# A transformer pair on one core: constant products put into seven more waits of TensorE

## The chip, the cores and the metric

The kernel runs on one core of one Trainium2 chip. The metric is the time on the device in microseconds (us) from the launch of the program to its end; smaller is better. A core has TensorE (matrix products, "PE" in the profile; its weight loads are "PEld"), VectorE ("DVE"), ScalarE ("ACT"), GpSimd ("POOL"), SyncE ("SP", here a queue that issues DMAs) and 16 DMA engines. TensorE reads from the on-chip memory SBUF and writes to eight banks of a second memory, PSUM, which the other engines read. TensorE's clock is granted at one of two levels, 2.4 GHz (the profile writes 1.00) and 1.2 GHz (0.50), and the profile tells which of them was granted over any stretch.

## The reference, cut to what matters

Everything is float32. Two different models are run one after the other on 512 tokens of width 1024:

```python
# first part: 2 layers on 16 meta tokens + 512 tokens
for l in range(2):
    u = rms_norm(h, ln_mix[l])
    (aq, ak, av, bq, bk, bv, cq, ck, cv, dq, dzf, dzb, di, dg, gz) = split_in(u @ w_in[l])
    y_a = windowed_sink_attention(...)     # softmax attention A, 4 heads
    y_b = axial_rope_attention(...)        # B
    y_c = differential_attention(...)      # C: two softmaxes, p1 - lam * p2
    y_d = hgrn2_bidirectional(...)         # linear attention, forwards and backwards
    merged = sum(sigmoid(gz)[n] * (y @ w_branch[l, n]) for n, y in ...)
    h = h + merged @ w_out[l]
    u = rms_norm(h, ln_ffn[l])
    h = h + (silu(u @ w_ffn_gate[l]) * (u @ w_ffn_up[l])) @ w_ffn_down[l]
x = rms_norm(h, ln_final)[meta:]
# second part: one layer, modulated by c
x = x + 0.5 * ga1 * rms_norm(swiglu(modulate(rms_norm(x, g), sh1, sc1), ...))
...                                        # window attention, S5 state space, w_out
x = x + 0.5 * ga3 * rms_norm(swiglu(modulate(rms_norm(x, g), sh3, sc3), ...))
```

The output is x. Nothing in the change touches a value of it.

## The kernel before, in words

Each engine has its own program, written out in order, and the programs meet at semaphores: `pe.wait_ge(S["x"], n)` holds TensorE's next instruction, and all behind it, until the counter x has reached n. TensorE's program is a fixed sequence. Activations lie with features on the partitions and the 528 tokens (16 meta, 512 others) along the free axis, in five token tiles (four of 128 and, last, the one of 16 meta tokens; `NT` is 5). A large product is done in three products of a high and a low half (`split_lin`, L1382 to L1384), with the weights streamed from HBM into a ring of slots; ScalarE makes the high half (L2243) and VectorE the low half (L2935) of each.

**The softmax attention** is `attention(first, end, turns, l)`, called once for each layer of the first part. It loops over steps n from `first` to `end + 1`. A step's unit `att[n]` is one pair of heads of one token tile of one kind; the kinds come in the order C, A, B, with 10 units each in layer 0 (so n is 0 to 29 and `end` is 30) and 8 each in layer 1, which has no meta tile left (30 to 53, `end` 54). In step n TensorE makes the scores of unit n (`scores`, L1644 and L1651), the values of unit n-2 (`values`, L1696 and L1710: these need the probabilities turned and copied out of PSUM by ScalarE, L2517), and turns the probabilities of unit n-1 (`turn_probs`, L1681 and L1684: after ScalarE's exponentials, L2503). Between them go `fill_piece`s, independent pieces of the input projection of 24 matmuls (L1733 to L1744), which give TensorE work while the others compute. The last two steps have no fill. Scores go to banks 0 to 3 (kinds A and B: banks 2(n mod 2) and the next); VectorE's minimum over them (L3285, semaphore `att_min`) frees them. `cell_end(n)` is the count of `att_min` at which unit n's scores have been read. The last unit of B ends in ScalarE's copy (L2526) and VectorE's scaling (L3359, `y_ready`).

**The linear attention** `linear_attention(ly)` first waits for that `y_ready`, then makes a `gate_piece` (L1835 to L1837: 24 matmuls of 264 or 256 columns and six more), then `head_stats` (L1807: matmuls of two columns), another gate piece, and so on. Its loop goes over units (d, t), direction and token tile; each has `sums` (L1880), two `pairs` (L1901), `outputs`, `state`, with gate pieces as fills (`fill`) between. `pairs(n, hp)` waits for factors that VectorE and GpSimd make (`g_query_x`, `g_key_x`; GpSimd's part is L500) and for `g_masked`, which says that banks 2 and 3 have been read. The unit (1, 4), direction 1 with the meta tile, is there in layer 0 alone, as its ninth.

**The second part's front** is `ffn(b2["ffn1"], ssm=True)`; its first two jobs are `pair_lin` (L1616 to L1619), which takes the eight tiles of x one by one as ScalarE (L2382) and VectorE (L2921) finish them, after the normalisation that ends the first part (`joint_means`, L1482 to L1487).

**Constant products.** `idle_products(bank, count)` multiplies `ident` (128x128) by 264 columns of constants into a bank that nothing reads before it is written anew:

```python
def idle_products(bank, count):
    for _ in range(count):
        mm(PS[:, bank, 0:264], ident, con[:, 0:264], start=True, stop=True)   # L1469
```

Before, it is called at the start of each layer only (L2013 to L2023), 62 matmuls in all.

Of the kernel before, what the change touches and what calls it, by code (L numbers as in the profile page):

```python
# [37 lines left out]
NT = len(TILES)  # L38
# [238 lines left out]
def build(nc, ins, out_dram):  # L277
    with ExitStack() as ctx:
# [259 lines left out]
        S = {n: sem(n) for n in names}  # L538
# [292 lines left out]
        layers = []  # L831
        x_there = [(x_loaded[k // 2], 16) for k in range(KT)]
        h_there = x_there
        for l in range(DEPTH):
            ly = dict(l=l)
# [112 lines left out]
        att, groups = [], []  # L948
# [94 lines left out]
        def cell_end(n):  # L1043

            return att[n]["cell0"] + len(att[n]["cells"])
# [319 lines left out]
        def _(pe):  # L1365
# [100 lines left out]
            def idle_products(bank, count):  # L1466

                for _ in range(count):
                    mm(PS[:, bank, 0:264], ident, con[:, 0:264], start=True, stop=True)  # L1469

            def mean_square(n):

                for i in range(len(n["tiles"])) if n["total"] is None else (0, KT - 1):
                    mean_tile(n, i)
# [129 lines left out]
            def pair_lin(js, x):  # L1604

                for j in js:
                    wait(pe, jobs[j.n - NB].freed)
                    pe.wait_ge(S["w_low"], j.loads[0].s + 1)
                for i in range(KT):
                    for part in range(2):  # L1610
                        wait(pe, x["is_low" if part else "is_high"][i])
                        for j in js:
                            (a, z), (wh, wl, xh, xl) = j.pieces[0], j.terms[i]
                            out = PB[j.buf][:, 0, 0:z - a]
                            if part == 0:
                                mm(out, wh, xh[:, a:z], start=i == 0, stop=False)  # L1616
                                mm(out, wl, xh[:, a:z], start=False, stop=False)
                            else:
                                last = mm(out, wh, xl[:, a:z], start=False, stop=i == KT - 1)  # L1619
                                if i == KT - 1:  # L1620
                                    last.then_inc(lin_full[j.buf], 1)
# [154 lines left out]
            def attention(first, end, turns=None, l=0, gated=False):  # L1776
                if gated:
                    scores(att[first])
                for n in range(first, end + 2):
                    if n < end and not gated:  # L1780
                        if n == turns:
                            pe.wait_ge(S["b_heads_ready"], NT * (l + 1))
                        scores(att[n])
                        made_scores[0] = n + 1
                    if first <= n - 2:
                        values(att[n - 2])
                    if first <= n - 1 < end:
                        turn_probs(att[n - 1], 0)
                        if second_bank(n - 1) != 4:
                            turn_probs(att[n - 1], 1)  # L1790
                    for f in fills_at.get(n, ()) if n < end else ():
                        fill_piece(f)
                    if gated:
                        if n + 1 < end:
                            scores(att[n + 1])
                        gated_step(n - first)
                    if first <= n - 1 < end and second_bank(n - 1) == 4:
                        turn_probs(att[n - 1], 1)
                    if turns and 0 <= n - layers[l]["turn_step"] < NT:
                        turn_heads(l, n - layers[l]["turn_step"])  # L1800
# [23 lines left out]
            def gate_piece(ly, q):  # L1824

                n, k, s, i = q // 16, q // 2 % KT, q % 2, NPIECE * ly["l"] + q
                ld, xu, xy = ly["gw"][q // 2], ly["xu"], ly["xy"][n]
                a, z = ly["cuts"][s]

                def terms(out, first, xs, seen=()):  # L1830
                    for m, (xh, xl) in enumerate(xs):
                        if seen:
                            wait(pe, seen[m])
                        wh, wl = high(ld)[:, first + m, :], low(ld)[:, first + m, :]
                        mm(out, wh, xh[:, a:z], start=m == 0, stop=False)  # L1835
                        mm(out, wh, xl[:, a:z], start=False, stop=False)  # L1836
                        last = mm(out, wl, xh[:, a:z], start=False, stop=m == len(xs) - 1)  # L1837
                    return last

                pe.wait_ge(S["w_low"], ld.s + 1)  # L1840
                if i:
                    pe.wait_ge(S["piece_gate"], i)
                terms(PS[:, 6, 0:z - a], 0, tiles_of(xu, range(KT)), xu["is_low"] if q == 0 else ()
                      ).then_inc(S["piece_full"], 1)
                if i:
                    pe.wait_ge(S["piece_read"], i)
                terms(PS[:, 7, 0:z - a], KT, tiles_of(xy, range(2)), xy["is_low"] if q % 16 == 0 else ()
                      ).then_inc(S["piece_branch"], 1)

            def linear_attention(ly):  # L1850
# [4 lines left out]
                pe.wait_ge(S["log_low"], NT * (l + 1))  # L1855
                pe.wait_ge(S["fill_read"], FILLS[l + 1])
                made = [3]
                gate_piece(ly, 0)
                head_stats("c", l, SQC, tiles[:NT - l])
                gate_piece(ly, 1)  # L1860
# [21 lines left out]
                                      RR[d][0:rows, 4 * i:4 * i + 4, 0:rows], start=x is LZH, stop=x is LZL)  # L1882
                    last.then_inc(S["g_sums"], 1)

                def pairs(n, hp):

                    u, d, t, a, z, rows = kept_of(n)
                    key, query = (0, HALF) if d == 0 else (HALF, 0)
                    pe.wait_ge(S["g_key_x"], 2 * u + hp + 1)
                    pe.wait_ge(S["g_query_x"], 2 * u + hp + 1)  # L1890
                    if 2 * u + hp:
                        pe.wait_ge(S["g_masked"], 2 * u + hp)
                    for plane in range(planes(rows)):
                        for b, w in blocks(rows):
                            for i in range(2):
                                out, lo = PS[b:b + w, 2 + i, HALF * plane:HALF * plane + w], HALF * i
                                if plane:
                                    x = y = EB[hp][lo:lo + HALF, plane - 1, b:b + w]
                                else:
                                    x, y = KF[lo:lo + HALF, hp, b:b + w], DQ[hp][lo:lo + HALF, a + b:a + b + w]  # L1900
                                last = mm(out, x, y, start=True, stop=True)  # L1901
                    if rows == P:
                        for i in range(2):
                            x = EB[hp][HALF * i:HALF * i + HALF, NLEV - 1, :]
                            last = mm(PS[key:key + HALF, 2 + i, HALF * NLEV:P * 4], x[:, key:key + HALF],
                                      x[:, query:query + HALF], start=True, stop=True)
                    last.then_inc(S["g_pairs"], 1)
# [42 lines left out]
                for n in range(len(units_of[l])):  # L1950
                    u, d, t, a, z, rows = kept_of(n)
                    if u:
                        pe.wait_ge(S["g_kf"], u)
                        pe.wait_ge(S["g_ez"], u)
                    for hp in range(2):
                        turn(PS[:, 5, 256 + P * hp:256 + P * hp + rows],
                             KTM[0:rows, t, 256 * d + P * hp:256 * d + P * hp + P], ident[0:rows, 0:rows])
                    mm(PS[0:rows, 5, 0:256], ZR[d][0:rows, 0:rows], LZH[0:rows, t, 256 * d:256 * d + 256],
                       start=True, stop=False)
                    mm(PS[0:rows, 5, 0:256], ZR[d][0:rows, 0:rows], LZL[0:rows, t, 256 * d:256 * d + 256],  # L1960
                       start=False, stop=True).then_inc(S["g_z"], 1)
                    sums(n, 0)
                    fill(n, 0)
                    if n:
                        if kept_of(n - 1)[5] == P:
                            outputs(n - 1, 1, HALF, False)
                        state(n - 1)
                    sums(n, 1)
                    fill(n, 1)
                    pairs(n, 0)  # L1970
                    fill(n, 2)
                    pairs(n, 1)
                    carried(n)
                    outputs(n, 0, 0, True)
                    fill(n, 3)
                    if rows == P:
                        outputs(n, 0, HALF, False)
                    fill(n, 4)
                    outputs(n, 1, 0, True)
# [2049 lines left out]
```

## Time and profile before

| what | value |
|---|---|
| time, median of 3 runs | 2984.65 us (2983.28 to 2986.08) |
| span of the profiled execution, first to last instruction | 2989.1 us |
| mean granted TensorE clock over that span | 0.992 |
| TensorE busy | 2927.0 us (98%) |
| VectorE, ScalarE, GpSimd busy | 1900.7 (64%), 1134.5 (38%), 377.3 us (13%) |

The time of the profiled execution as a whole is not given; what is known of it is its span of 2989.1 us, which is 4.45 us above the median of the timed runs.

How to read the rows below. In a timeline a row gives start and duration in us, engine, line and operation, tiles, shape, the number of instructions merged into the row, and in brackets the engine's idle time before it with what ended that. A matmul's duration includes its way through the pipeline, so the cost of one of several is the distance of their starts, or the row's duration over its count. In a table of stretches a row gives the stretch in us, its length, then for PE, PEld, DVE, ACT and POOL the busy time with the number of instructions, then the granted TensorE clock (1.00 is 2.4 GHz), the DMA engines' share and GB/s. Where the table was asked for PE alone, only PE's column stands before the clock.

### The profile page before, as it was taken

The page shows a single profiled execution, that of the slowest core. Times are in us where ns is not written, and L with a number is a line of the kernel's source. Part 1 is how long each engine was busy: PE and PEld are TensorE (multiplying, and loading weights), DVE is VectorE, ACT ScalarE, POOL GpSimd, SP SyncE. Part 2 cuts the span into 40 slices and gives each one's busy share as a digit, 9 for nine tenths or more (in the row PEclk, how much of TensorE's full clock was granted, in tenths as well). Part 3 has the DMA queues.
Part 4 walks back from the last instruction along what each step waited for, and adds up shares of the span by engine and source line. Part 5 has one row for each costly group of instructions (what it writes and reads, how often), then busy time and mean ns, then how long its engine had stood idle before and what let it go on. Part 6 is the DMA issues. An engine that isn't in the chain of part 4 may idle for free.

```text
span 2989.1 us, 56782 instructions
## 1 busy us (share of the span) xinstructions
PE 2927.0 (98%) x23600; PEld 2632.0 (88%) x23600; DVE 1900.7 (64%) x3660; ACT 1134.5 (38%) x2022; POOL 377.3 (13%) x610
## 2 busy tenths in 40 slices
PE   9999999999999999999999999999999999999998
PEld 8777999999999998789999899987888885799997
DVE  5564677557777746646865766677536655685565
ACT  4655233232212235552323434434222222554353
POOL 0242433000000020323320000002000000000000
PEclk9999999999999999999999999999999999999999
DMA  6725766244555574347533444438723431134442
GB/s 207 212 49 143 182 149 165 73 141 158 196 189 169 196 213 127 72 131 190 148 114 121 151 143 152 162 115 214 185 93 135 141 121 43 57 115 157 148 174 85
DMA packets 119511, 428.65 MB, mean 143 GB/s; under 512 B 14248, under 2 KB 16680, under 8 KB 114264
## 3 DMA queue, kind: packets, MB, share of 16 engines
q1 hardware_dynamic: 67032, 261.50, 25.6%
q0 software_dynamic: 52224, 163.51, 20.7%
q8 instruction: 189, 3.10, 0.4%
q14 instruction: 66, 0.54, 0.1%
HBM read 414.34 MB, written 109.01 MB: 175 GB/s over the span
## 4 chain that ended last, share of the span: by engine, by line
PE 88%; DVE 4%; ACT 4%; issue 2%; DMA 1%; POOL 1%; SPq 0%; DVEq 0%; ACTq 0%; POOLq 0%
PE acc L1382 13%; PE acc L1383 13%; PE acc L1384 13%; PE acc L1835 5%; PE acc L1836 5%; PE acc L1837 5%; PE acc L2101 4%; PE acc L2102 4%; PE acc L2103 4%; ACT temps L2503 2%; PE acc L1710 2%; PE acc L1651 1%; PE acc L1417 1%; PE acc L2119 1%; PE acc L1901 1%
## 5 line engine op out<-in xcount | busy, mean ns | idle before, releaser
L2243 ACT ACTIVATE toep_r<-ring 128x1024 fp32r<-128x1024 f32 (+2 forms) x216 | 251.4, 1165 | 327.6 <-PE acc L1384 327.6
L1383 PE MATMUL acc<-normed_r,toep_r 128*128 128x264 f32 (+2 forms) x1120 | 357.0, 319 | 0.0
L2935 DVE TENSOR_TENSOR ring_r<-ring,toep_r 128x1024 fp32r<-128x1024 f32 (+2 forms) x212 | 289.4, 1366 | 96.1 <-ACT toep_r L2243 95.5
L1384 PE MATMUL acc<-work_r,ring_r 128*128 128x264 f32 (+2 forms) x984 | 323.6, 329 | 0.0
L1835 PE MATMUL acc<-residual_r,toep_r 128*128 128x264 f32 (+1 forms) x1024 | 301.0, 294 | 1.6 <-DVE mixed L3359 1.6
L1836 PE MATMUL acc<-normed_r,toep_r 128*128 128x264 f32 (+1 forms) x1024 | 292.2, 285 | 0.0
L1837 PE MATMUL acc<-residual_r,ring_r 128*128 128x264 f32 (+1 forms) x1024 | 291.3, 284 | 0.0
L1382 PE MATMUL acc<-work_r,toep_r 128*128 128x264 f32 (+2 forms) x828 | 268.4, 324 | 0.6 <-DVE ring_r L2945 0.6
L1383 PE MATMUL acc<-work_r,toep_r 128*128 128x264 f32 (+2 forms) x720 | 231.5, 321 | 0.0
L1383 PEld LDWEIGHTS acc<-normed_r,toep_r 128*128 128x128 f32 x1120 | 210.6, 188 | 14.5
L1835 PEld LDWEIGHTS acc<-residual_r,toep_r 128*128 128x128 f32 x1024 | 195.5, 191 | 8.0 <-DVE mixed L3359 1.9
L1382 PE MATMUL acc<-mixed_r,toep_r 128*128 128x264 f32 x704 | 202.5, 288 | 0.0
L1384 PEld LDWEIGHTS acc<-work_r,ring_r 128*128 128x128 f32 x984 | 185.1, 188 | 17.3
L1384 PE MATMUL acc<-mixed_r,ring_r 128*128 128x264 f32 x704 | 199.5, 283 | 0.0
L1836 PEld LDWEIGHTS acc<-normed_r,toep_r 128*128 128x128 f32 x1024 | 195.7, 191 | 1.5
L2649 ACT ACTIVATE toep<-acc 128x264 f32<-128x264 f32 (+1 forms) x128 | 49.6, 388 | 386.8 <-PE acc L1837 386.8
L1837 PEld LDWEIGHTS acc<-residual_r,ring_r 128*128 128x128 f32 x1024 | 196.1, 192 | 0.0
L1382 PEld LDWEIGHTS acc<-work_r,toep_r 128*128 128x128 f32 x828 | 155.7, 188 | 13.7 <-issue 1.2
L1382 PE MATMUL acc<-temps_r,toep_r 128*128 128x512 f32 (+1 forms) x416 | 157.0, 377 | 0.7 <-DVE ring_r L2935 0.7
L1384 PE MATMUL acc<-temps_r,ring_r 128*128 128x512 f32 (+1 forms) x416 | 155.4, 374 | 0.0
L2503 ACT ACTIVATE temps<-temps,small 128x528 f32<-128x528 f32 (+6 forms) x176 | 113.3, 644 | 91.0 <-DVE small L3285 90.8
L1383 PEld LDWEIGHTS acc<-work_r,toep_r 128*128 128x128 f32 x720 | 135.4, 188 | 10.5
(614 smaller groups left out, 8117.3 us busy)
## 6 DMA issues: line engine op xcount, KB each, us to landing
ring<-in_w_pair SPq DMA_DIRECT2D x120, 512.0 KB, 3.8
sums_store<-in_w_pair POOLq DMA_DIRECT2D x80, 512.0 KB, 8.8
ring<-in_w_gb SPq DMA_DIRECT2D x64, 640.0 KB, 4.5
ring<-in_w_down SPq DMA_DIRECT2D x32, 704.0 KB, 4.2
lower_store<-in_w_pair POOLq DMA_DIRECT2D x20, 1024.0 KB, 10.4
sums_store<-sums_store POOLq DMA_DIRECT2D x40, 512.0 KB, 5.1
extra<-in_w_ada POOLq DMA_DIRECT2D x18, 1024.0 KB, 6.0
toep<-in_w_ada POOLq DMA_DIRECT2D x18, 1024.0 KB, 6.3
```

The source lines that it names most:

```text
L1382: mm(out, wh, xh[:, a:z], start=i == 0, stop=False)
L1383: mm(out, wh, xl[:, a:z], start=False, stop=False)
L1384: last = mm(out, wl, xh[:, a:z], start=False, stop=end)
L1835: mm(out, wh, xh[:, a:z], start=m == 0, stop=False)
L1836: mm(out, wh, xl[:, a:z], start=False, stop=False)
L1837: last = mm(out, wl, xh[:, a:z], start=False, stop=m == len(xs) - 1)
L2101: mm(out, wh, xh, start=begins and k == 0, stop=False, skip_group_check=True)
L2102: mm(out, wh, xl, start=False, stop=False, skip_group_check=True)
L2103: last = mm(out, wl, xh, start=False, stop=k == 3, skip_group_check=True)
L2243: A(high(ld), slot(ld), ACT.Copy).then_inc(S["w_high"], 1)
L2503: A(x, x, ACT.Exp, bias=negm[0:rows, i:i + 1], scale=-1.0, accum_out=sums[0:rows, i:i + 1]).then_inc(S["att_exp"], 1)
L2935: V.tensor_tensor(low(ld), slot(ld), high(ld), ALU.subtract).then_inc(S["w_low"], 1)
```

## The change

`idle_scores(n, count)` is new: it waits until the scores of unit n have been read and then puts `count` constant products into the first of their banks. Constant products are added in seven places, 31 matmuls in all. `pairs` waits for `g_masked` first instead of last. Nothing is taken away, and no other engine's program is changed.

```diff
+            def idle_scores(n, count):
+                pe.wait_ge(S["att_min"], cell_end(n))
+                idle_products(2 * (n % 2), count)
...
 def pair_lin(js, x):                      # second part's front
                 for j in js:
                     wait(pe, jobs[j.n - NB].freed)
                     pe.wait_ge(S["w_low"], j.loads[0].s + 1)
+                idle_products(2 * js[0].buf, 5)
                 for i in range(KT):
...
 def attention(...):
                 for n in range(first, end + 2):
+                    if n == first + 1 and not gated:
+                        if l:
+                            pe.wait_ge(S["y_ready"], layers[0]["groups"])
+                        idle_products(6, 3)
+                    if n == end + 1 and not gated:
+                        idle_scores(end - 2, 3)
                     if n < end and not gated:
                         ...
                         scores(att[n])
...
                         if second_bank(n - 1) != 4:
                             turn_probs(att[n - 1], 1)
+                    if n == layers[l]["A"][0] and l == 0 and not gated:
+                        idle_scores(n - 1, 3)
+                    if n == end and not gated:
+                        idle_scores(end - 1, 2)
                     for f in fills_at.get(n, ()) if n < end else ():
...
 def linear_attention(ly):
                 pe.wait_ge(S["y_ready"], ly["groups"])
                 ...
                 made = [3]
+                idle_scores(ly["B"][1] - 1, 2)
                 gate_piece(ly, 0)
...
-                def pairs(n, hp):
+                def pairs(n, hp, unread=0):
+                    if 2 * u + hp:
+                        pe.wait_ge(S["g_masked"], 2 * u + hp)
+                    if unread:
+                        idle_products(2, unread)
                     pe.wait_ge(S["g_key_x"], 2 * u + hp + 1)
                     pe.wait_ge(S["g_query_x"], 2 * u + hp + 1)
-                    if 2 * u + hp:
-                        pe.wait_ge(S["g_masked"], 2 * u + hp)
...
-                    pairs(n, 0)
+                    pairs(n, 0, 3 if (d, t) == (1, NT - 1) else 0)
```

## Rows read from the trace of the kernel before

**Rows 1.** The page's parts 1 and 4: busy time; chain that ended last, by engine.
```profile
PE 2927.0 (98%) x23600; PEld 2632.0 (88%) x23600; DVE 1900.7 (64%) x3660; ACT 1134.5 (38%) x2022; POOL 377.3 (13%) x610
PE 88%; DVE 4%; ACT 4%; issue 2%; DMA 1%; POOL 1%; SPq 0%; DVEq 0%; ACTq 0%; POOLq 0%
```
**Rows 2.** The view of cores: span and mean granted TensorE clock.
```profile
core 0: 2989.1 us, clock 0.992
```
**Rows 3.** Table of stretches, all engines: the seven at 1.2 GHz inside the span.
```profile
174.50:181.20 6.70, 6.70 (x46) 6.24 (x43) 6.10 (x19) 1.72 (x7) 3.42 (x4) 0.50 0.00 1
...
287.20:297.30 10.10, 9.51 (x82) 9.22 (x81) 0.67 (x2) 1.89 (x6) 0.00 (x0) 0.50 0.01 2
300.80:304.10 3.30, 3.30 (x17) 3.30 (x16) 0.00 (x0) 0.00 (x0) 3.30 (x2) 0.50 0.00 0
...
505.60:512.30 6.70, 5.99 (x45) 5.98 (x46) 3.42 (x17) 0.00 (x0) 4.02 (x9) 0.50 0.63 193
1160.95:1164.30 3.35, 2.88 (x14) 2.83 (x15) 3.28 (x12) 1.94 (x5) 0.00 (x0) 0.50 0.01 2
1314.55:1317.90 3.35, 3.35 (x27) 2.61 (x23) 0.22 (x2) 0.77 (x1) 2.44 (x1) 0.50 0.03 5
2027.95:2031.30 3.35, 3.35 (x8) 2.66 (x9) 3.35 (x6) 1.88 (x3) 0.00 (x0) 0.50 1.11 198
```
**Rows 4.** Timeline of PE, the kernel's start: constant products that are already there.
```profile
3.21 5.34 PE L1469 MATMUL acc<-con 128*128 128x264 f32 x14 [3.21 <-DMA con<-in_consts]
9.12 3.83 PE L1469 MATMUL acc<-con 128*128 128x264 f32 x16 [0.57 <-ACT work L2200]
```
**Rows 5.** Timeline of PE, front of layer 1's softmax attention: unit 31's scores, unit 30's turns.
```profile
1158.17 0.43 PE L1644 MATMUL acc<-con,work 128*128 128x64 f32 x2 [0.52 <-DVE small L3285]
...
1161.42 0.59 PE L1681 MATMUL acc<-con,temps 128*16 128x128 f32 x2 [1.74 <-DVE temps L3301]
```
**Rows 6.** Table of stretches, PE alone: like stretches of layer 0 and of layer 1.
```profile
107.73:112.03 4.30, 4.12 (x35) 1.00 1.06 129
1161.42:1166.68 5.26, 5.26 (x35) 0.72 0.00 0
107.73:129.70 21.97, 20.85 (x201) 1.00 0.73 155
1161.42:1183.63 22.21, 21.80 (x201) 0.93 0.12 39
```
**Rows 7.** Timeline of PE, layer 0, step 10: second half of unit 9's turns; next fill.
```profile
172.78 0.39 PE L1684 MATMUL acc<-con,temps 16*128 16x16 f32 x4 [1.07 <-ACT mixed L2517]
...
176.42 0.55 PE L1742 MATMUL acc<-toep_r,residual_r 128*128 128x256 f32 x1
```
**Rows 8.** Timeline of PE, layer 0's last units and the first gate piece.
```profile
286.99 0.98 PE L1710 MATMUL acc<-mixed,work 128*64 128x16 f32 x16 [1.26 <-ACT mixed L2517]
...
289.22 0.61 PE L1696 MATMUL acc<-con,small 16*64 16x16 f32 x8
289.76 1.04 PE L1710 MATMUL acc<-mixed,work 128*64 128x16 f32 x16
...
291.72 0.59 PE L1835 MATMUL acc<-residual_r,toep_r 128*128 128x264 f32 x1 [0.59 <-DVE mixed L3359]
```
**Rows 9.** Timeline of PE, layer 1's last units.
```profile
1314.26 1.77 PE L1710 MATMUL acc<-mixed,work 128*64 128x128 f32 x16 [2.01 <-ACT mixed L2517]
...
1318.41 0.66 PE L1696 MATMUL acc<-con,small 128*64 128x128 f32 x8
1319.45 1.09 PE L1710 MATMUL acc<-mixed,work 128*64 128x128 f32 x16 [0.38 <-ACT mixed L2517]
```
**Rows 10.** Timeline of PE, layer 0's linear attention, ninth unit: pairs and gate piece.
```profile
506.31 0.45 PE L1901 MATMUL acc<-work 64*16 64x16 f32 x20 [1.12 <-POOL work L500]
506.69 0.59 PE L1835 MATMUL acc<-residual_r,toep_r 128*128 128x264 f32 x1
```
**Rows 11.** Timeline of PE, the second part's front: the first product.
```profile
2027.86 0.73 PE L1616 MATMUL acc<-temps_r,toep_r 128*128 128x512 f32 x1 [2.21 <-ACT temps_r L2382]
```

## The prediction

> **What bounds the kernel now.** I read the page's busy times and its chain first. TensorE is busy 98% of the span and holds 88% of the chain that ended last [rows 1]; the reader should take from this that the end moves with TensorE's own work and with the few microseconds in which it stands still, and that nothing is won on another engine unless TensorE waits for it. Then the view of cores: the mean granted clock is 0.992 over 2989.1 us [rows 2], so about 0.008 x 2989.1 x 2 = 48 us passed at 1.2 GHz. The table of stretches finds those inside the span [rows 3]: seven, together 36.9 us, for 35.1 us of which TensorE is busy; the rest, as far as the rounding goes, lies at the very end, where TensorE has nothing left to do. All seven begin in or just behind a wait or a run of very small matmuls. The timelines around them show what TensorE did before the clock fell, and what each new product will lie beside.
>
> What is to be had at most follows from rows 3. Where TensorE runs dense products at 1.2 GHz, half of the busy time would go. Where it runs small matmuls less goes: the 16 matmuls of L1710 took 1.77 us at 1.2 GHz and 1.09 us at 2.4 [rows 9]. All seven stretches gone would save about 3.0 (174.5) + 3.5 (287.2) + 1.6 (300.8) + 2.8 (505.6) + 1.0 (1161) + 1.4 (1314.6) + 1.6 (2028) = 14.9 us. TensorE's page in the Trainium skill ("TensorE: Matmul & The Clock Gate", Terms) prices it otherwise: the throttled time times one minus the clock's share. By that page the same 36.9 us would be worth an estimated 18.4 us; the L1710 rows disagree (0.68 us saved of 1.77, where the page gives 0.89), because small matmuls are paced by more than the clock.
>
> **The price of a product.** 16 constant products took 3.83 us at 2.4 GHz, 0.24 us each; 14 at the start, where the clock was still low, took 5.34 us, 0.38 us each [rows 4]. I take these two. 31 products are 7.4 us at 2.4 GHz if nothing hides them. The waits added are all for things read long before: `att_min` of a unit whose turns are already made, layer 0's `y_ready` in layer 1, `g_masked` of a mask whose outputs are already under way. I cost the waits at nothing; behind them in TensorE's queue is everything, so if one was late its whole lateness would be on the path.
>
> **The seven places.**
>
> *Step first+1, both layers, 3 products (0.72 us).* They go before the scores of the second unit, which stand 0.52 us idle for VectorE's minimum [rows 5]; a little more is hidden by the tail of the fill before it, so they end at most 0.2 us late. The scores themselves are followed by 1.74 us of idleness that ends with VectorE's work on the unit before [rows 5]. The 0.2 is thus hidden there: cost 0. In layer 1 the clock fell at the end of that second wait, 0.5 us ahead of the turns; in layer 0, with the same waits, it did not. The two layers price the fall: from the turns to the next scores it is 4.30 us in layer 0 and 5.26 in layer 1, 0.96 us more; but at the next wait for VectorE's L3301 it is 21.97 against 22.21, 0.24 us more [rows 6], since VectorE, not TensorE, set that point and TensorE waited less for it. The gain lies between 0.2 and 1.0; I take 0.3.
>
> *Step A[0], layer 0, 3 products.* They go into the 1.07 us before the second half of unit 9's turns [rows 7]. 0.72 us is hidden wholly: cost 0. The clock fell 1.7 us later [rows 3], after a stretch of matmuls of 16 columns. From 176.42 to 181.2 the fill ran dense at 1.2 GHz [rows 7], so 4.8 / 2 = 2.4 us are to be had, and 0.6 in the small ones before. If the three products hold the clock, up to 3.0; the steps behind it wait now and then for ScalarE, so I take 2.4 when it is held; and I take it as held at 6 in 10: 1.4.
>
> *End of the softmax attention, 2 + 3 products, and 2 more before the first gate piece.* Here I argue against the change. The waits that stand out, 1.26 us in layer 0 and 2.01 us in layer 1, are before the values of the last unit but one [rows 8, 9]. The new products come behind these values and behind the last unit's turns, immediately one after the other, before L1696. In layer 0 there is no idle time between L1696 and the last values [rows 8]: five products are 5 x 0.38 = 1.9 us, all on the path, as the clock is already low from 287.2 on. In layer 1 L1696 is followed by 0.38 us of idleness for ScalarE's copy [rows 9], so 1.2 - 0.4 = 0.8 us are on the path. The last two stand behind the wait for `y_ready`, not in it, so nothing hides them: 0.8 us in layer 0 at 1.2 GHz, 0.5 in layer 1. Against that, seven products in a thin stretch let the clock come back sooner after the fall, before the gate pieces: from 291.72 to 297.3, 5.6 us, these ran at 1.2 GHz, and a start that is 2.7 us later leaves about 2.9 us of them there: 1.3 us won back. Layer 0: 2.7 - 1.3 = +1.4, between -0.8 (clock back before the last values) and +2.7; I take +1.0. Layer 1: the stretch at 1.2 GHz ends before the new products: +1.3, between 0 (a fall behind it is avoided in other executions) and +1.3; I take +1.2. The stretch at 300.8 follows the two-column matmuls of `head_stats`; no product is put there: 0, and between -1.6 and 0.
>
> *pairs, unit (1, 4), 3 products.* They go into the 1.12 us for GpSimd [rows 10], hidden; cost 0. The clock fell 0.7 us before that wait ended [rows 3], so only about half of the products can come before it. The gate piece from 506.69 to 512.3 ran at 1.2 GHz [rows 10]: 2.8 us if held. Even chances: 1.4 less a little for the unit's own latencies, 1.2.
>
> *pair_lin, 5 products (1.2 us).* They go into the 2.21 us before the first product, hidden. The clock fell 0.1 us behind that wait [rows 11, 3]. Eight products of 512 columns took 3.35 us there, 0.42 us each where half would do: 1.6. VectorE, which makes the tiles, was busy for all of the 3.35 us too [rows 3], so it could hold TensorE up once that is faster; I take 1.5, between 0.3 and 1.7.
>
> **The sum.** -0.3 -1.4 +1.0 +1.2 -1.2 -1.5 = -2.2 us; with some relief for stretches that fall in other executions (layer 0's front did not fall in this one) I put it at -2.5. The sum is made against the profiled span of 2989.1 us, which would become 2986.6; that execution lies 4.45 us above the median, and as the clock falls at somewhat different places in each, I carry the difference to the median: 2984.65 - 2.5 = 2982.1.
>
> **The rivals.**
>
> *All of it works (0.25).* The clock is held at all four waits that are filled, and the products at the ends of the softmax attention bring it back early or keep it up. For it: four of the seven falls stand at waits that are filled, and two more at the ends. Against it: at both ends the longest wait stays empty. Gains 1.0 + 3.0 + 2.8 + 1.6, layer 0's end -0.8, the stretch at 300.8 -1.6, layer 1's end 0: about -10.8, or 2974; a milder form of it, -7, gives 2977.6.
>
> *The others take over (0.20).* TensorE gets to its next wait sooner and stands longer there, as in rows 6, where three quarters of the loss was gone 22 us later. Then the gains shrink to a quarter except in the second part's front: -0.25 -0.6 -0.6 -1.5 + 2.2 = -0.8: 2983.9.
>
> *The ends decide (0.15), slower than before.* The seven products at the end of each softmax attention are on the path at full price, 2.7 + 1.3 = 4.0 us, the clock comes back no sooner, and the filled waits hold the clock only in the second part's front (-1.5) or not even there. For it: the place of the products behind the long wait, and 287.2 to 297.3 at 1.2 GHz already. It decides as soon as fewer than two of the three other stretches are saved. +2.5 to +4.0: 2987.2 to 2988.7, and past 2990.6 only where the later start brings one more fall onto dense work (another 1.6 to 3).
>
> *The products don't move the clock at all.* It is within the last one; the constant products at the kernel's start ran from 0.38 down to 0.24 us each as the clock was granted [rows 4], which speaks against it. It would leave the costs alone, +2.2 to +4.0.
>
> **The numbers.** The forecast's own case has 0.40. Changes under 0.2% (6 us) can hardly be told from none here. Faster by over 0.2%, under 2978.7: most of the first rival and a little of the forecast's, 0.26. Slower by over 0.2%: 0.06. Within: 0.68. The range of 8 in 10 goes from 2975.5 to 2987.5.
>
> **What would show it.** In the profile after: at 2027 to 2031 a clock of 1.00 and products of L1616 0.23 us apart; 31 more matmuls of L1469; the idle times before L1644 in the front and before L1684 at 172, L1901 at 506 and L1616 at 2027 filled; at the ends the last values starting 0.7 us or more later behind the turns than before, and the first gate piece two products behind `y_ready`. I am wrong if the ends cost nothing (then ScalarE's copy or VectorE ended last there), if the clock falls again a few microseconds behind a filled wait, or if the mean granted clock stays at 0.992.

## The result: 0.19% slower

Over 21 runs of each on the same chips the changed kernel took 2992.44 us in the median (2989.25 to 2999.96) and the kernel before 2987.38 us (2980.82 to 2995.20). The ratio is 1.0019, with a 95% interval of 1.0013 to 1.0025: 5.7 us slower, 3.9 to 7.5. The forecast was 2982.1 us, 0.09% faster than the 2984.65 us of the three runs shown then, in a range up to 2987.5. The sign was wrong. (Those three runs of before were also low ones: with more of them its median is 2987 to 2989 us. This moves both kernels alike and is not the error: 5.7 us on top of 2984.65 would be 2990.4, outside the range too.)

The clock did what was hoped for. The mean granted clock, averaged over the runs, rose from 0.9925 (34 runs of before) to 0.9958 (21 runs of the change): 2 x 0.0075 x 2988 = 45 us at 1.2 GHz became 25 us. Twenty microseconds of low clock went, and the kernel became slower. So the products cost more than they brought.

The profile after, first the view of cores and TensorE's line of the page's part 1, which answer to [rows 1, 2]:

```profile
core 0: 2990.6 us, clock 0.996
```
```profile
PE 2933.3 (98%) x23662; PEld 2635.4 (88%) x23662; DVE 1900.7 (64%) x3660; ACT 1134.2 (38%) x2022; POOL 376.2 (13%) x610
```

The other engines are unchanged. TensorE has 62 more instructions than in [rows 1], not 31. The view of line L1469 in the trace of before, and then in that of after, says why (after the count: shortest, median and longest duration in ns, then the first and last start in us):

```profile
L1469 PE MATMUL acc<-con x62: 386/386/809, 3.2 to 1075.8; 128*128 128x264 f32 x62
```
```profile
L1469 PE MATMUL acc<-con x124: 384/386/807, 3.5 to 2033.0; 128*128 128x264 f32 x124
```

Before, the code calls `mm` on this line 31 times (7 + 4 x 2 + 6 in layer 0, 2 + 8 in layer 1), and the trace has 62 matmuls. A product of two full float32 operands is two instructions here. The change adds 31 calls of `mm`, which the description of it counts as 31 matmuls, and thus 62 instructions of 0.24 us: **a call costs 0.48 us, not 0.24.** The row that I took the price from said x14 where the code beside it says 7.

The stretches at 1.2 GHz that the profile after has inside its span, in the table of stretches (columns as in [rows 3]), and two stretches that lost theirs:

```profile
287.70:291.00 3.30, 3.30 (x10) 2.54 (x10) 0.00 (x0) 0.38 (x3) 0.00 (x0) 0.50 0.02 5
301.35:304.70 3.35, 3.35 (x17) 3.35 (x16) 0.00 (x0) 0.00 (x0) 3.35 (x3) 0.50 0.00 0
506.15:509.50 3.35, 3.35 (x30) 2.33 (x29) 3.24 (x18) 0.00 (x0) 2.64 (x7) 0.50 0.14 49
1160.95:1164.30 3.35, 3.03 (x27) 3.04 (x28) 3.17 (x11) 2.10 (x6) 0.00 (x0) 1.00 0.00 0
1315.10:1318.40 3.30, 3.30 (x17) 2.77 (x14) 0.00 (x0) 1.45 (x3) 2.85 (x1) 0.50 0.00 0
1366.30:1369.65 3.35, 3.35 (x19) 3.35 (x17) 1.85 (x10) 0.00 (x0) 3.35 (x11) 0.50 0.47 92
2027.95:2035.00 7.05, 6.54 (x23) 3.99 (x22) 3.60 (x6) 3.58 (x6) 4.05 (x4) 1.00 0.93 177
```

Seven stretches of 36.9 us became five of 17 us. The falls at 174, 1161 and 2028 are gone, those at 287 and 506 are shorter, those at 301 and 1315 are as they were, and there is a new one at 1366. Each profile is one execution; which of these differences are the change's is read from all thirteen profiles, at the end of the experiments. The stretch at 287.7 holds nothing but ten instructions of L1469: the clock was low while the kernel multiplied constants.

**The ends of the softmax attention**, in the timeline of after, layer 0 (answering to [rows 8]):

```profile
286.31 0.65 PE L1716 MATMUL acc<-mixed,work 128*64 128x16 f32 x16 [1.26 <-ACT mixed L2536]
...
287.75 4.12 PE L1469 MATMUL acc<-con 128*128 128x264 f32 x10
291.80 0.41 PE L1702 MATMUL acc<-con,small 16*64 16x16 f32 x8
...
293.59 1.16 PE L1469 MATMUL acc<-con 128*128 128x264 f32 x4 [0.59 <-DVE mixed L3378]
294.39 0.48 PE L1851 MATMUL acc<-residual_r,toep_r 128*128 128x264 f32 x1
```

and layer 1 (answering to [rows 9]):

```profile
1313.85 1.09 PE L1716 MATMUL acc<-mixed,work 128*64 128x128 f32 x16 [2.01 <-ACT mixed L2536]
...
1317.44 2.90 PE L1469 MATMUL acc<-con 128*128 128x264 f32 x10
1320.28 0.66 PE L1702 MATMUL acc<-con,small 128*64 128x128 f32 x8
...
1323.18 1.16 PE L1469 MATMUL acc<-con 128*128 128x264 f32 x4 [1.01 <-DVE mixed L3378]
```

The reader should see three things. The long waits, 1.26 and 2.01 us, stand exactly as before; the products come after them. Ten instructions take 4.12 us where the clock is low and 2.90 where it comes back on the way, 0.8 and 0.6 us a call. And four more stand behind the wait for `y_ready`. The first gate piece starts at 294.39 where before it started at 291.72, although the values before it started 0.68 us earlier: 3.35 us lost up to there. The earlier rise of the clock gave back 2.4: the matmuls of `head_stats` behind the gate piece start at 298.23, against 297.99 before, 0.9 us late by the same measure. In layer 1 the values start 0.41 us earlier than before and the gate piece (1323.98 against 1321.92) 2.06 later, 2.5 us lost.

**The overfull waits**, in the timeline of after (to [rows 7, 10, 11]):

```profile
172.60 1.60 PE L1469 MATMUL acc<-con 128*128 128x264 f32 x6
174.13 0.42 PE L1690 MATMUL acc<-con,temps 16*128 16x16 f32 x4
...
505.70 2.65 PE L1469 MATMUL acc<-con 128*128 128x264 f32 x6
508.28 0.45 PE L1920 MATMUL acc<-work 64*16 64x16 f32 x20
...
2031.04 2.39 PE L1469 MATMUL acc<-con 128*128 128x264 f32 x10
```

Three calls fill 1.5 us where the wait had 1.07, and 2.6 us where it had 1.12, since there the clock fell in their midst. These waits are gone from the profile, as forecast. I had the first two filled to two thirds, and they ran over by 0.4 and 1.4 us; in the second part's front ten instructions took 2.39 us in a wait of 2.21, and the first product came no later behind L1492 (before, L1487) than before. In the front of the softmax attention the scores came 0.66 us later behind the fill, but the wait behind them shrank from 1.74 to 1.18 us, so the turns came no later: cost 0, as forecast.

### The profile page after: what moved, and what is told of

Same layout as the page of the kernel before. It is cut to its first block, busy times and chain, and to the rows that moved or that the text cites. A ratio compares the mean times of both kernels' runs of the same rounds, so it can differ in the third digit from the quotient of the medians.

```text
span 2990.6 us, 56906 instructions
## 1 busy us (share of the span) xinstructions
PE 2933.3 (98%) x23662; PEld 2635.4 (88%) x23662; DVE 1900.7 (64%) x3660; ACT 1134.2 (38%) x2022; POOL 376.2 (13%) x610
## 4 chain that ended last, share of the span: by engine, by line
PE 88%; DVE 5%; ACT 4%; issue 2%; DMA 1%; POOL 1%; SPq 0%; DVEq 0%; ACTq 0%
PE acc L1382 13%; PE acc L1383 13%; PE acc L1384 13%; PE acc L1851 5%; PE acc L1852 5%; PE acc L1853 5%; PE acc L2120 4%; PE acc L2121 4%; PE acc L2122 4%; ACT temps L2522 2%; PE acc L1716 2%; PE acc L1657 1%; PE acc L1417 1%; PE acc L2138 1%; PE acc L1897 1%
## 5 line engine op out<-in xcount | busy, mean ns | idle before, releaser
L2954 DVE TENSOR_TENSOR ring_r<-ring,toep_r 128x1024 fp32r<-128x1024 f32 (+2 forms) x212 | 287.7, 1358 | 95.5 <-ACT toep_r L2262 94.9
L1383 PEld LDWEIGHTS acc<-normed_r,toep_r 128*128 128x128 f32 x1120 | 210.6, 188 | 14.5
```

The source lines that it names most:

```text
L2954: V.tensor_tensor(low(ld), slot(ld), high(ld), ALU.subtract).then_inc(S["w_low"], 1)
```

## The experiments

All ratios are against the kernel before, with 95% intervals, from 5 rounds each; "clock" is the mean granted clock over a kernel's runs. `pairs` waits for `g_masked` first in every one of these kernels, also in those that are otherwise the kernel before with one addition (e7, e8). In the runs of before beside them it was 0.9923 to 0.9930.

**e1: the waits alone.** The three lines at the ends are taken out of the change.

```diff
-                    if n == end + 1 and not gated:
-                        idle_scores(end - 2, 3)
-                    if n == end and not gated:
-                        idle_scores(end - 1, 2)
-                idle_scores(ly["B"][1] - 1, 2)
```

> The change without its products at the ends of the softmax attention (2 + 3 before the last values, 2 before the first gate piece); the fillings of the front, of step A[0], of pairs and of pair_lin stay, 17 calls. After the result (0.19% slower) three theories stand. PRICE: one call of idle_products is two matmul instructions (the trace of before has 62 for 31 calls), 0.48 us at 2.4 GHz and 0.76 at 1.2, so the ends cost twice what I took, all on the path, and the fillings still win. It expects 0.05 to 0.15% faster than before here (2 to 4 us), that is 7 to 9 us below the whole change. FEW FALLS: the profiled execution of before had more clock falls than most, so there is little for the fillings to win: within 0.05% of before. OTHERS: the fillings themselves do the harm, overfull waits (3 calls are 1.4 us in a wait of 1.07 or 1.12 us) or waits moved to other engines: 0.1% slower or more.

Measured: 0.9992 (0.9983 to 1.0000), median 2984.97 us against 2989.20, clock 0.9957. That is inside PRICE's range. The interval holds FEW FALLS' range too (within 0.05% of before); what speaks against FEW FALLS is its premise: over 34 runs the mean clock of before is 0.9925, so the profiled execution with its 0.992 was an ordinary one. OTHERS is refuted: the fillings don't harm. And the clock is that of the whole change (0.9957 against 0.9958): the fourteen calls at the ends bring no clock on top.

**e2: the ends alone.** The fillings in the front, at step A[0], in `pairs` and in `pair_lin` are taken out, the ends stay.

> The kernel before with only the products at the ends of the softmax attention, seven calls in each layer. PRICE: 7 x 0.76 = 5.3 us in layer 0 less 2 to 3 won back by an earlier rise of the clock, 7 x 0.48 to 0.76 less 0.4 idle in layer 1 = 3 to 5, less 1: 5 to 7 us slower, 0.17 to 0.23%. FEW FALLS: the same sum, 4 to 6 us. OTHERS: 0 to 2 us slower, under 0.07%.

Measured: 1.0018 (1.0009 to 1.0028), 5.4 us slower, clock 0.9937. Inside PRICE's range (and FEW FALLS', which has the same sum here); OTHERS expected under 0.07%. The ends alone are as slow as the whole change. Against e1 the change is 0.27% slower (1.0019 to 0.9992), 8 us for the same 14 calls, 0.58 us each. That they cost less alone may be because they then win some clock (0.9937 against 0.9925), but the two figures, 5.4 and 8 us, lie within each other's uncertainty.

**e5: the ends doubled.** As e2, each count twice.

```diff
-                        idle_scores(end - 2, 3)
+                        idle_scores(end - 2, 6)
-                        idle_scores(end - 1, 2)
+                        idle_scores(end - 1, 4)
-                idle_scores(ly["B"][1] - 1, 2)
+                idle_scores(ly["B"][1] - 1, 4)
```

> As e2 with the three counts at the ends of the softmax attention doubled, 4 + 6 before the last values and 4 before the first gate piece: 14 calls in each layer where e2 has 7. After the first four runs PRICE leads: a call is 0.48 us at 2.4 GHz and all on the path. The seven more calls in each layer run mostly when the clock is up again: 2 x 7 x 0.48 = 6.7 us above e2, +0.22% on top of its +0.18%, so +0.36 to +0.42%. Rival HIDDEN (the calls at the ends are partly hidden and e2's loss comes from more clock falls behind them): +0.20 to +0.30%. If a call cost what I took (0.24 us), +0.29%.

Measured: 1.0051 (1.0038 to 1.0064) in 5 runs, clock 0.9932. The point is above what each theory expected; the interval reaches into PRICE's range (0.36 to 0.42%) and stays clear of the other two. The 14 further calls cost 0.33%, 9.9 us or 0.7 us each, with an uncertainty of about 0.35 us on that. The timeline of e5, the last calls before each layer's last values:

```profile
289.51 7.06 PE L1469 MATMUL acc<-con 128*128 128x264 f32 x20
...
1321.85 4.62 PE L1469 MATMUL acc<-con 128*128 128x264 f32 x20
```

Twenty instructions, ten calls: 7.06 and 4.62 us. In layer 1, with the clock up, that is 0.46 us a call and 0.23 an instruction. HIDDEN and the price that I had taken are both refuted. The calls of the trace also add up to the loss: from their first start to the start of what follows it is 7.00 and 4.55 us for these twenty and 1.69 us in each layer for the four behind `y_ready`, less the 0.4 us of idleness that they fill in layer 1: 14.5 us, and 0.51% is 15.2 us, with a mean clock hardly above that of before (0.9932 against 0.9930). So the excess over PRICE is, in this trace, the 0.7 us that each of layer 0's ten calls took where the clock was down for most of them.

**e3: the products put into the wait that was left empty.** As e1, and two calls in layer 0, four in layer 1, ahead of the values of the last unit but one.

```diff
+                    if n == end and not gated:
+                        idle_scores(end - 2, 2 if l == 0 else 4)
                     if first <= n - 2:
                         values(att[n - 2])
```

> As e1, and 2 calls (layer 0) and 4 calls (layer 1) in the wait that the change leaves empty, ahead of the values of the last unit but one (1.26 and 2.01 us idle in the trace of before). PRICE: 2 x 0.48 fit into 1.26, 4 x 0.48 into 2.01; where they hold the clock the falls at 287 and 1315 go, 1 to 4 us below e1: 0.1 to 0.25% faster than before. FEW FALLS: not much different from e1, up to 2 us below. OTHERS: no gain over e1, or a loss.

Measured: 0.9980 (0.9971 to 0.9989), median 2982.32 us, clock 0.9963. Within PRICE's range. The timeline of e3 (layer 0, then layer 1):

```profile
283.94 1.16 PE L1469 MATMUL acc<-con 128*128 128x264 f32 x4
285.27 0.65 PE L1716 MATMUL acc<-mixed,work 128*64 128x16 f32 x16 [0.18 <-issue]
...
1304.84 1.95 PE L1469 MATMUL acc<-con 128*128 128x264 f32 x8
1307.01 1.09 PE L1716 MATMUL acc<-mixed,work 128*64 128x128 f32 x16 [0.23 <-issue]
```

The waits of 1.26 and 2.01 us are down to 0.18 and 0.23, and the values don't start later for it. The table of stretches of e3:

```profile
284.00:288.50 4.50, 3.77 (x63) 3.04 (x62) 0.76 (x3) 1.85 (x10) 0.00 (x0) 1.00 0.01 4
288.65:292.00 3.35, 3.35 (x16) 3.35 (x17) 0.38 (x1) 1.05 (x2) 0.00 (x0) 0.50 0.00 0
...
1305.00:1313.00 8.00, 6.48 (x67) 4.71 (x65) 2.07 (x5) 4.79 (x11) 2.90 (x1) 1.00 0.00 0
```

In layer 1 the clock stays up through the end. In layer 0, whose last units are matmuls of 16 columns, it still falls, here for 3.4 us. That isn't shown to be the filling's doing: the profile of e10, the same kernel, has 6.7 us there, and that of e8, which puts nothing there, has 3.3. The tables of stretches of e10 and e8:

```profile
287.20:293.90 6.70, 6.11 (x43) 5.97 (x40) 0.67 (x2) 1.38 (x3) 0.00 (x0) 0.50 0.01 2
290.10:293.40 3.30, 2.88 (x13) 2.88 (x14) 0.67 (x2) 1.25 (x3) 0.00 (x0) 0.50 0.02 5
```

In e3's profiled execution the fall at 288.65 is the only one before the last 10 us of the span; it was also the fastest of e3's 11 runs, 2977.4 us. That of e10 has five.

**e4: every count cut to what its wait holds**: 1, 2, 2 and 4 calls for 3, 3, 3 and 5, and e3's.

> As e3, with every count cut to what its wait holds at 0.48 us a call: 1 call in the front (0.52 us), 2 at step A[0] (1.07), 2 at pairs (1.12), 4 at pair_lin (2.21), 2 and 4 at the ends. PRICE: up to 1.5 us below e3 where the overfull waits cost (0.4 us at A[0] and up to 1.4 at pairs in the profile of after), unless the fewer products let the clock fall again: 0.1 to 0.3% faster than before. FEW FALLS: 0 to 0.05% faster. OTHERS: better than e3 by 1 to 2 us, since less is overfull.

Measured: 0.9986 (0.9977 to 0.9994), clock 0.9957. No better than e3, rather the other way, within the uncertainty. I had expected up to 1.5 us of gain. That what is saved on overfull waits is paid back in clock would fit the two clocks (0.9957 against 0.9963), but these lie within their scatter: not shown.

**e7: e3's addition alone**, on the kernel before (with the order of waits in `pairs` changed).

> The kernel before with only the products in the longest wait at the end of the softmax attention, ahead of the values of the last unit but one: 2 calls in layer 0, 4 in layer 1. PRICE (what fits into a wait costs nothing, and may hold the clock): -0.03 to -0.12%, what e3 has over e1 (0.12%) with its uncertainty. Rival: e3's lead over e1 was chance: 0 to +0.05%, since the clock falls a little later all the same.

Measured: 0.9995 (0.9984 to 1.0005), clock 0.9942. The point lies in PRICE's range, but the interval holds both theories: not decided by the time. The clock, 0.9942 against 0.9930, is hardly outside its scatter.

**e8: pair_lin's five calls alone** (and the order of waits in `pairs`).

> The kernel before with only the five calls of pair_lin. In the profile of after this place won 2.4 us against before. PRICE: 5 x 0.48 = 2.4 us in a wait of 2.2, the clock held: -1.6 to -2.4 us, -0.05 to -0.08%. OTHERS (VectorE takes it back at its next weight split): -0.02 to 0%.

Measured: 0.9997 (0.9987 to 1.0008), clock 0.9938. Inconclusive, between the two ranges: less than 2 us can't be told apart so. The single pieces of the gain were too small to be measured one at a time; together they are measured. The changed order of waits in `pairs` was never run by itself; e7 and e8 both have it and neither is slower than before by more than 0.08% at the end of its interval, so it is not what makes the change slower.

**e6: the change at the price that I had taken.** In the attention layers each call makes two one-instruction products instead of one float32 product:

```diff
+                for _ in range(2 * count):
+                    mm(PS[:, bank, 0:264], HR[:, 0, 0:P], HR[:, 0, 0:264], start=True, stop=True)
```

> The whole change, but each of the calls inside the attention layers (26 of the 31) makes two products of 264 columns in the short form that the fills use (one instruction each, about 0.12 us, both operands from the rounded activations) instead of one in full float32 (two instructions, 0.24 us each). So a call costs 0.24 us, the price that I took. The numbers of instructions and all waits are those of the change. PRICE: the ends then cost about half, 3 to 4 us less than the change, which comes out at my own sum: -0.02 to -0.12% against before. Rival PLACE (what counts is that something stands there at all: the waits, the order of pairs, clock falls), as the change: +0.1 to +0.2%.

Measured: 1.0011 (1.0001 to 1.0020), clock 0.9941. A miss: I had expected a gain. The ends did become cheaper; the timeline of e6, the ten short products before layer 0's last values, at low clock, where the change had 4.12 us:

```profile
290.64 2.57 PE L1479 MATMUL acc<-residual_r 128*128 128x264 f32 x10
```

But the clock was held less. The table of stretches of e6:

```profile
172.50:182.60 10.10, 10.10 (x70) 8.99 (x69) 8.33 (x25) 3.18 (x15) 4.46 (x4) 0.50 0.09 34
288.60:298.70 10.10, 9.51 (x82) 8.98 (x80) 0.67 (x2) 1.89 (x6) 0.00 (x0) 0.50 0.01 2
```

At step A[0], where the change lost its fall, there are 10 us at 1.2 GHz again. So my sum would have been wrong at my own price, too: with the cheap products the gain that I set against it didn't come.

**e9: the waits alone, with short products.**

> As e1 (the fillings without the ends), with the products inside the attention layers in the short form of e6: 9 of... all calls but pair_lin's five take half as long. e6 came out at +0.11% where I had expected a gain; its profile has the clock falling for 10 us at 172 and at 288, and the mean clock over its runs is 0.994 where the change has 0.996. Theory HOLD: a filling that stands in its wait for half as long holds the clock less, so the halved price is paid back in clock: -0.02 to +0.05% against before and a mean clock of 0.993 to 0.995. Rival NOISE (e6 was drawn high): as e1, -0.05 to -0.12%, clock 0.9955 to 0.9965.

Measured: 0.9996 (0.9987 to 1.0004), clock 0.9933 over 12 runs, against e1's 0.9957 over 11. The time lies between the ranges of the two theories; the clock is in HOLD's (0.993 to 0.995) and outside NOISE's. The times of e1 and e9 alone don't part, the clocks do. The short products differ from the others in two things, in how long they take and in their operands (rounded activations instead of constants); which of the two lets the clock fall no run here parts. e6 and e9 together give the ends at half the price: 1.0011 to 0.9996, 0.15% or 4.5 us, where the full price had 8 us (the change against e1). That is in proportion, though each of the two has an uncertainty of 3 to 4 us. The table of stretches of e9 has the same two falls as e6:

```profile
173.00:183.10 10.10, 10.10 (x70) 8.99 (x69) 8.17 (x25) 3.03 (x15) 4.61 (x5) 0.50 0.06 22
289.00:299.20 10.20, 9.61 (x82) 9.32 (x80) 0.67 (x2) 1.99 (x7) 0.00 (x0) 0.50 0.01 2
```

**e10: e3 again.**

> e3 once more, word for word, for a second estimate of the version that beats both kernels: -0.12 to -0.24% if e3's -0.20% holds; nearer to e1's -0.08% if a part of it was chance.

Measured: 0.9977 (0.9967 to 0.9987), median 2983.71 against 2989.08 us, clock 0.9963. e3 stands: some 0.2%, 6 to 7 us, faster than the kernel before, and 0.4% faster than the change.

**e11: e3 overfilled**, 4 and 5 calls instead of 2 and 4.

> As e3, with 4 and 5 calls in the longest wait at the end of each softmax attention instead of 2 and 4: 1.9 us into 1.26 and 2.4 into 2.01, so about 0.7 + 0.4 us more on the path. PRICE: 0 to 1.1 us above e3 (0 to 0.04%), as what is overfull is paid in full, less a little clock. If overfilling were what made the change slower rather than the place of its products, this would be 0.1% or more above e3.

Measured: 0.9983 (0.9973 to 0.9993), clock 0.9965. PRICE's range above e3 and e10 (0.03 to 0.06%, inside the uncertainty). Three more calls at this place, about 1.1 us more than its waits hold, cost nothing that could be measured; overfilling as such is not what made the change slower, its 14 calls at the ends are.

**All thirteen profiles, place by place.** The lengths, in us, for which the granted clock was 1.2 GHz in each profile (the rows above cut them at 0.05 us and so show them a little shorter). At the two ends, "filled" means calls ahead of the values of the last unit but one, as in e3; "short" are e6 and e9.

| place | not filled | filled | short |
|---|---|---|---|
| second part's front | 3.4 in before, e2, e5, e7 | none in nine (after, e1, e3, e4, e6, e8 to e11) | |
| step A[0] | 6.8 in before, e2, e5, e7, e8 | none in after, e1, e3, e4, e11; 3.4 in e10 | 10.2 in both |
| `pairs`, unit (1, 4) | 6.8 in before, e7; 3.4 in e2, e5; none in e8 | 3.4 in after, e1, e10, e11; none in e3, e4 | 3.4 in e9, none in e6 |
| front of layer 1 | 3.4 in before; none in e2, e5, e7, e8 | none in after, e1, e3, e10, e11; 3.4 in e4 | none |
| layer 0's end | 10.2 in before, e6, e9; 6.8 in e1, e5; 3.4 in after, e2, e8 | 3.4 in e3, e7, e11; 6.8 in e4, e10 | |
| layer 1's end | 3.4 in seven of eight (not in e5) | none in five (e3, e4, e7, e10, e11) | |

Three places part well: the second part's front, layer 1's end where the calls stand in the wait, and step A[0], where e10 alone has a fall with the filling, a shorter one. The front of layer 1 doesn't: its fall at 1161 in the profile of before stands in none of the profiles of the other four kernels that leave it empty, so I had booked the gain of a fall that is rare.

## Why the prediction was wrong

- **The price of a product: mis-sized by two, and this is the step that failed.** "16 constant products took 3.83 us at 2.4 GHz, 0.24 us each", and the same for 14 at low clock. These were instructions, two to a call. A call is 0.48 us and some 0.8 at 1.2 GHz (e5: 0.46 at full clock, 0.7 a further call over its runs). The whole sum used 0.24 and 0.38. With the calls at 0.48 and 0.8 and all else as I had it, the ends are 5.0 to 5.6 less 1.3 won back in layer 0 and 3.0 in layer 1, and the sum of -2.2 becomes +2.3 to +2.9: the sign turns. With the fillings at what e1 measured, -2.4 instead of -4.4, it is +4.3 to +4.9, inside the 3.9 to 7.5 measured.
- **The ends: mechanism right, size wrong.** I had them on the path, behind the long waits and behind `y_ready`: so they are. The semaphores added cost nothing, as I had it: at the ends only `y_ready`, which was waited for before, has idle time ahead of L1469. I took +1.0 and +1.2 us; alone they cost 5.4 (e2), on top of the fillings 8 (e1 against the change). With 0.48 and 0.8 the working gives 5 x 0.8 + 2 x 0.48 to 0.8 in layer 0 and 5 x 0.48 + 2 x 0.48 - 0.4 in layer 1: 5.0 to 5.6 and 3.0 before what the clock gives back. In layer 0's profile the two errors met, 3.35 lost less 2.4 back = +0.9 for my +1.0; in layer 1 it was 2.5 for 1.2. That my figure for layer 0 came out in this profile is luck.
- **The four fillings: a gain, but by the point a smaller one.** My terms were -0.3 -1.4 -1.2 -1.5 = -4.4 us; e1 measured -2.4, between 0 and -5, so they aren't refuted. Part of the difference is the waits that I took as hiding all of 0.72 us and that three calls overran, by 0.4 us at A[0] and 1.4 at `pairs`.
- **VectorE's point in the front: right.** In the profile after the stretch from layer 1's first turns to the next wait for VectorE's L3301 (now L3320) is 21.96 us, and in layer 0, too; before, 22.21 and 21.97 [rows 6]. The table of stretches of after, PE alone:

```profile
1161.27:1183.23 21.96, 20.85 (x201) 1.00 0.12 45
108.70:130.66 21.96, 20.86 (x201) 1.00 0.73 153
```

  In this pair of profiles a fall that slows the stretch by 0.96 us at first is worth 0.25 us in the end.
- **How falls were priced.** The low clock's time, halved, is not what can be had: 19 us of it went in e1 (0.9925 to 0.9957), which halved would be 9.6 us, and 2.4 us of time went, 4.2 with the overrun of 1.8 added back. The runs of the kernel before give a price that needs no change at all: a line through the times of its 34 runs against their time at 1.2 GHz rises by 0.31 us for each microsecond (standard error 0.03; 0.33 and 0.32 in the two later sets of 29; each run's clock is given to 0.001, which is 6 us). I had taken 14.9 of 36.9 us, 0.40. At 0.31 the books nearly close: e3 should win 7.0 less 1.8 of overrun, 5.2 us, and won 6.0 and 6.9 (e10); the change should lose 8.0 to 8.6 at the ends and 1.8 of overrun less 0.31 x 20, 3.6 to 4.2 us, and lost 5.7, between 3.9 and 7.5. The page of the Trainium skill that I set beside ("TensorE: Matmul & The Clock Gate", Terms) prices it at that half; e1 and these 34 runs disagree, by more than I had allowed.
- **The rivals.** "The ends decide" came nearest, at a chance of 0.15: the ends are on the path and the kernel is slower. Its conditions did not come true, as the clock did come back sooner at layer 0's end and step A[0] was held. It was priced at +2.5 to +4.0 with the half price; at 0.48 and 0.8 a call it would be +6.5 to +8.6. "The products don't move the clock at all" is refuted by the mean clock, 0.9925 to 0.9958. I gave 0.06 to slower by over 0.2%; it came out right at this bound.

What stays open: why the profiled before and after differ by only 1.5 us in span where the medians differ by 5.1 (single executions of a kernel scatter over 10 us or more, as the falls come at other places in each), what each filled wait is worth in time by itself, and the 1.5 to 2 us by which the change is slower than the sum above, which its uncertainty of 1.8 us may or may not explain.

## What to carry to other kernels

Before pricing an instruction from a row, hold the row's count against the number of times that the code makes it: a call can be two instructions, and the price is that of the call. Work that holds the clock must stand inside the wait, ahead of the instruction that waits; the same products a few instructions later are plain extra work on the bound engine, and e3 against the change is 0.4% for nothing but their place and number. Price a saved microsecond of low clock from the scatter of the kernel that you have, time against clock over many runs; here that gave about a third of its length, not half. And look at several profiles before you book a fall as one to be saved.

## What the runs showed of the hardware that was not expected

- A matmul of two float32 operands on L1469, 128x128 by 264, ran as two instructions of 0.23 to 0.24 us; one of the rounded operands of the same shape as one, 0.12 us at 2.4 GHz (e9) and 0.25 at 1.2 (e6). A full float32 call cost four of the short ones.
- Six one-instruction products of 0.12 us in a wait where six of 0.24 had stood did not keep the clock up: at step A[0] it fell for 10.2 us in both profiles with them (e6, e9), for 6.8 in the five without any, and in one of six with the longer ones (3.4, e10); over the runs the mean clock was 0.9933 (e9) instead of 0.9957 (e1).
- Where the clock falls is not fixed. In layer 0's front, where before and e2 have the same instructions, the profile of e2 has a fall and that of before none [rows 6: 1.00 from 107.73]; and e3 and e10, the same kernel, have one fall and five. The table of stretches of e2:

```profile
108.10:111.40 3.30, 3.30 (x18) 3.30 (x17) 2.59 (x8) 2.68 (x8) 0.00 (x0) 0.50 1.12 143
```

  And 34 runs of before had clocks from 0.989 to 0.996 and times from 2982.6 to 2995.9 us, longer where the clock was lower.
